# Expert up weights in two 4 MB loads instead of four of 2 MB

## The chip, the cores and the metric

The kernel runs on one core of one Trainium2 chip. The metric is device time in microseconds of one execution; before the change it is 2763.34 us, the median of three executions (2761.53 to 2763.45).

## What is computed

A first block of two layers (SwiGLU feed-forward, a mixer of convolution, gated recurrence and pooling, cross attention, a second feed-forward, a layer norm after each), then a second block of one layer, whose mixture of experts is the part that matters here. All is float32; T = 256 tokens, D = 1024, 32 experts of which each token uses 4. Cut to what matters:

```
h = layer_norm_2(DEEPNORM_ALPHA * h + y @ w_out, ln1_g, ln1_b)      # norm "A" in the kernel
# moe: router logits -> top 4 of 32 experts per token, softmaxed gates; for every expert e, on its tokens
hdn    = xb @ w_up[e] + b_up[e]                  # w_up[e]: 1024 x 2048, 8 MB
gate_h = minimum(hdn[:, :1024], 7);  up_h = clip(hdn[:, 1024:], -7, 7)
act    = (up_h + 1) * gate_h * sigmoid(1.702 * gate_h)
y      = (act @ w_down[e] + b_down[e]) * gate    # w_down[e]: 1024 x 1024, 4 MB
h = layer_norm_2(DEEPNORM_ALPHA * h + sum of y, ln2_g, ln2_b)       # norm "B"
h = h + sigmoid(h @ w_ple_gate + b_ple_gate) * (p @ w_ple)
```

## The kernel before

One program with a queue of instructions for each engine, tied by counting semaphores that the code writes out itself; nothing reorders them. SyncE (SP) issues nearly all loads, in the order in which they stand in its block. They land in a ring of 12 slots (`ring`, 8 KB per partition and slot, so 1 MB a slot): `loaded[s]` counts loads of slot s that landed, `used[s]` releases by the engine that read it. A load waits until its slot has been given back, and all that stands behind it on SP waits with it. `align()` moves on to slot 0.

Ahead of the experts the ring holds, in slots 0 to 5, the parameters of norm A (released by GpSimd), the router weights (TensorE), a table `tri` (VectorE, L1836), a table `before` (VectorE, at L1850, after the counting matmuls of L927), `b_up` (TensorE, L902) and `b_down` (TensorE, L915). Slots 6 to 11 are free long before.

Each expert then fills the ring exactly once: 8 slots for w_up, 4 for w_down. `load_pair` fills two adjacent slots with one transfer of 2 MB, in which each of the 128 partitions gets 16 KB that are adjacent in memory; it waits for both slots. Since partition p of k-tile pair j gets rows 256j + 2p and 256j + 2p + 1 of w_up, the other operand has to be cut the same way: `strip("A", k)` takes every second column of `hn` (transposes of norm A) and of `h` (the gather), and the router weights and the norm's gains and biases (`COLS_EVEN_ODD`) are laid out in the same order.

Every expert has room for 64 tokens (`few`, the branch that runs here; `many` is for fuller experts). TensorE's work for one expert, in order (counted as the trace does, which records each float32 matmul instruction twice): 64 up matmuls (L963), 8 for each slot k, with a wait for the transfer ahead of slots 0, 2, 4 and 6 and a release behind each slot; four transposes (L976); the gather of the next expert's tokens by a 0/1 matrix (32 matmuls, L935); four more transposes (L976); the combine of the previous expert's result (L944); two transposes of the gates (L990); 32 down matmuls (L1001), with waits ahead of slots 8 and 10. VectorE and ScalarE turn up into down's input between. After the last expert come the final combine, norm B, and a gate product with loads that follow the expert loads on SP.

Of the kernel before, what the change touches and what calls it, by code (L numbers as in the profile page):

```python
# [23 lines left out]
P = 128  # L24
# [3 lines left out]
DT = D // P  # L28
LAYERS = 2
FF = 2816  # L30
CH = 256
# [17 lines left out]
         ("conv_b_2", 8), ("lru_b_r_2", 8), ("lru_b_i_2", 8), ("lru_lambda_2", 8),  # L49
         ("gla_b_gate_2", 4), ("gla_norm_g_2", 2)]  # L50
COLS3 = [("ln2_g_2", 8), ("ln2_b_2", 8)]
COLS_EVEN_ODD = {"ln1_g_2": 0, "ln1_b_2": 4}


Q, K, PR, SU, FQ, FK, AA, AX_, V, Y = 0, 1024, 2048, 3072, 4096, 5120, 6144, 7168, 7680, 9728
# [99 lines left out]
def program(nc, book, a):  # L155

    book.iters = {}
    with ExitStack() as ctx:
# [11 lines left out]
        work_halves, at = {}, 0  # L170
        for off, size in sorted(((DH_, 2048), (HTH, 2048), (HDL, 1024), (HDH, 1024), (HTL, 2048), (GH_, 2048), (UH_, 2048))):
# [3 lines left out]
            at = off + size  # L175
# [74 lines left out]

        def col(name, i, n=1):

            if name in COLS_EVEN_ODD:
                at = 16 + 8 * (i % 2) + COLS_EVEN_ODD[name] + i // 2
                return cols[:, 2, at:at + 1]
            for b, group in enumerate((COLS1, COLS2, COLS3)):
                at = 0
                for nm, rows in group:
                    if nm == name:
                        if isinstance(i, int):  # L260
                            return cols[:, b, at + i:at + i + n]
                        return cols[:, b, bass.ds(i + at, n)]
                    at += rows
# [22 lines left out]
        def _(sp):  # L286
# [27 lines left out]
                plain(sp)  # L314
                sp.dma_start(dst, src).then_inc(loaded[s].sem, 16)

            def load_pair(name, second, src):

                s = pos[0] % RING
                pos[0] += 2  # L320
                loaded[s].add(name)
                for x, i in ((name, s), (second, s + 1)):
                    used[i].add(x)
                    slot_of[x] = i
                    sp.wait_ge(used[i].sem, used[i].at(x))
                    plain(sp)
                sp.dma_start(ring[:, s:s + 2, :].rearrange("p s n -> p (s n)"), src).then_inc(loaded[s].sem, 16)

            def align():
                pos[0] = -(-pos[0] // RING) * RING  # L330
# [115 lines left out]
            for j in range(4):  # L446
                load(f"w2o{j}", rows(wout2, 2 * j), "p (k n) -> p k n", k=2)
            ln_params(("lnp", "A"), a["ln1_g_2"], a["ln1_b_2"], 0)
            load("router", a["w_router_2"].rearrange("a (k p r) n -> p (a k) (r n)", p=P, r=2),
                 "p (k n) -> p k n", k=4)  # L450
            load("tri", a["c_tri"], None)
            load("before", a["c_moe"].rearrange("p a n -> p (a n)"), None)
            load("bup", a["b_up_2"].rearrange("a e (j n) -> (a e j) n", n=512), None)
            load("bdown", a["b_down_2"].rearrange("a e n -> (a e) n"), None, part=32)
            align()
            wup = a["w_up_2"].rearrange("a e (k p r) n -> p (a e) k (r n)", p=P, r=2)
            wdn = a["w_down_2"].rearrange("a e (j p r) n -> p (a e) j (r n)", p=P, r=4)
            with counted(book, sp, "e", EXPERTS, loaded + used) as e:
                for k in range(0, DT, 2):
                    load_pair(("moe", "u", k), ("moe", "u", k + 1), wup[:, e, k // 2, :])  # L460
                for j in range(0, 4, 2):
                    load_pair(("moe", "d", j), ("moe", "d", j + 1), wdn[:, e, j // 2, :])
            ln_params(("lnp", "B"), a["ln2_g_2"], a["ln2_b_2"], 0)
            load("ptok", a["p_2"].rearrange("l a (t p) n -> p (l a t) n", p=P), "p (t n) -> p t n", t=TT)
            load("wple", rows(a["w_ple_2"].rearrange("a k n -> (a k) n"), 0), "p (k n) -> p k n", k=2)
# [7 lines left out]
        def _(pe):  # L473
# [62 lines left out]

            def strip(tag, k):

                return bass.ds(CH * (k // 2) + k % 2, P, step=2) if tag == "A" else slice(k * P, k * P + P)

            def transposes(tag, src, ready):

# [136 lines left out]
            open_bank(0, "params")  # L679
            for b, n in enumerate((128, 102, 16)):  # L680
                pe.transpose(ps[:, 0, b * P:b * P + n], work[0:n, Y + b * P:Y + b * P + P], ident[0:n, 0:n])
            for r in range(2):
                mm = pe.transpose(ps[:, 0, 272 + 8 * r:280 + 8 * r], work[0:8, bass.ds(Y + 384 + r, P, step=2)],
                                  ident[0:8, 0:8])
            mm.then_inc(pe_full.add("params"), 1)

            with counted(book, pe, "L", LAYERS, emptied + [pe_full]) as L:
# [261 lines left out]
            def few():  # L949
                pe.wait_ge(h_ready.sem, h_ready.at(("h", "A")))  # L950
                pe.wait_ge(sel_ready.sem, sel_ready.at("sel0"))
                gather("xg0")
                with counted(book, pe, "few", EXPERTS, emptied + [pe_full], "e") as e:
                    def gate_up():

                        for x in range(2):
                            open_bank(x, ("gu", x))
                        pe.wait_ge(emptied[2].sem, emptied[2].at("xg"))
                        for k in range(DT):
                            s = arrived(("moe", "u", k)) if k % 2 == 0 else slot_of["moe", "u", k]  # L960
                            for x in range(2):
                                for lo, c0 in ((0, 0), (CAP, D)):
                                    mm = pe.matmul(ps[lo:lo + CAP, x, :],  # L963
                                                   work[:, XG + k * CAP:XG + k * CAP + CAP],
                                                   ring[:, s, c0 + 512 * x:c0 + 512 * x + 512],
                                                   start=(k == 0), stop=(k == DT - 1))
                                if k == DT - 1 and x == 0:
                                    mm.then_inc(pe_full.add(("gu", 0)), 1)
                            mm.then_inc(used[s].sem, 1)

                    def turned(x):

                        pe.wait_ge(emptied[x].sem, emptied[x].at(("gu", x), 1))
                        emptied[x].add(("gut", x))
                        for f in range(4):
                            mm = pe.transpose(ps[:, x, f * P:f * P + P],  # L976
                                              work[:, bass.ds(GUT + 512 * x + f, P, step=4)], ident[:])
                        mm.then_inc(pe_full.add(("gut", x)), 1)

                    gate_up()  # L980
                    turned(0)
                    pe.wait_ge(sel_ready.sem, sel_ready.at("sel"))
                    gather("xg")
                    turned(1)

                    combine("back")

                    open_bank(2, "GT")
                    for t in range(TT):
                        mm = pe.transpose(ps[:, 2, t * P:t * P + P], work[:, GG + t * P:GG + t * P + P], ident[:])  # L990
                    mm.then_inc(pe_full.add("GT"), 1)

                    open_bank(3, "y")
                    for j in range(4):
                        if j % 2 == 0:
                            pe.wait_ge(dve_done.sem, dve_done.at(("few", j // 2)))
                        s = arrived(("moe", "d", j)) if j % 2 == 0 else slot_of["moe", "d", j]
                        for kk in range(2):
                            f = 2 * j + kk
                            for half in range(2):  # L1000
                                mm = pe.matmul(ps[half * CAP:half * CAP + CAP, 3, :],  # L1001
                                               work[:, ACTS + f * CAP:ACTS + f * CAP + CAP],
                                               ring[:, s, kk * D + half * 512:kk * D + half * 512 + 512],
                                               start=(f == 0), stop=(f == DT - 1))
                        mm.then_inc(used[s].sem, 1)
                pe.wait_ge(emptied[3].sem, emptied[3].at("y", 1, few=EXPERTS - 1))
                combine("last")

            def many():
                with counted(book, pe, "many", EXPERTS, emptied + [pe_full], "e") as e:  # L1010
                    def gate_up(j):

                        for what, bank, c0 in (("g", 2 * (j % 2), 0), ("u", 2 * (j % 2) + 1, D)):
                            open_bank(bank, ("all", what, j))
                            for pt in range(2):
                                o = c0 + 512 * (j // 2) + 2 * (j % 2) + pt
                                for k in range(DT):
                                    s = slot_of["moe", "u", k]
                                    if (j, what, pt, k % 2) == (0, "g", 0, 0):
                                        arrived(("moe", "u", k))  # L1020
                                    mm = pe.matmul(ps[:, bank, pt * T:pt * T + T], ring[:, s, bass.ds(o, P, step=4)], hT[:, k, :],
                                                   start=(k == 0), stop=(k == DT - 1))
                                    if (j, what, pt) == (3, "u", 1):
                                        mm.then_inc(used[s].sem, 1)
                            if (j, what) != (3, "u"):
                                mm.then_inc(pe_full.add(("all", what, j)), 1)
# [60 lines left out]
        def _(act):  # L1087
# [24 lines left out]
                    row(nm, b, at)  # L1112
                    at += n

            for nm, at in COLS_EVEN_ODD.items():
                act.dma_start(work[at:at + 4, Y + 384:Y + 640], a[nm].rearrange("a (k n) -> (a k) n", n=CH))\
                    .then_inc(prm.add(("row", nm)), 16)
            row("ln2_g_2", 2, 0)
            row("ln2_b_2", 2, 8)
# [983 lines left out]
```

## Time and profile before

| what | us |
|---|---|
| median of three executions | 2763.34 |
| the profiled execution | 2764.23 |
| its span (first to last instruction) | 2762.4 |
| TensorE matmul busy | 2585.3 (94%) |
| VectorE, ScalarE, GpSimd busy | 855.3, 648.1, 147.4 |
| mean granted clock of TensorE | 0.964 |
| bytes read | 663.02 MB |

Durations below are of the profiled execution, and its own time is the one to hold them against; it was 0.89 us longer than the median. The page cuts the span into 40 equal slices of 69 us. TensorE's busy share is modelled, so a 9 doesn't say by itself that TensorE is the limit. A matmul group's mean (595 ns at L963) is longer than the distance between two starts, because they overlap in pairs; distances are read from start times.

### The profile page before, as it was taken

Reading aid. Unit: us, or ns where it says so; the run is one execution under the profiler, and the core shown is the slowest. Engines: PE = TensorE matmul, PEld = TensorE weight load, DVE = VectorE, ACT = ScalarE, POOL = GpSimd, SP = SyncE. Lnnn points to the kernel's source line nnn. Section 1 sums busy time; section 2 is a strip of 40 time slices with the busy share of each in tenths; the row PEclk is TensorE's granted clock in tenths of the full one; section 3 lists DMA queues with packets and bytes.
Section 4 is the critical chain, followed back from the end, with each engine's and each line's share of the span. In section 5 each row is a group of like instructions: output and inputs, shape, how many; then the busy total and the mean of one; then the engine's idle time right before and its main releaser. Section 6 shows DMA issues by size and latency. Waiting matters only on the chain. (4 is left out here: it accounts for less than half of the span.)

```text
span 2762.4 us, 34575 instructions
## 1 busy us (share of the span) xinstructions
PE 2585.3 (94%) x13461; PEld 1769.7 (64%) x13461; DVE 855.3 (31%) x1274; ACT 648.1 (23%) x799; POOL 147.4 (5%) x101
## 2 busy tenths in 40 slices
PE   7999998999899999889999897999999999999987
PEld 7997756699799785669976784444444444444433
DVE  4442321344444241234431535111111211211222
ACT  4330011233333101123312311121221221221211
POOL 0001300100100130110010101000000000000001
PEclk9999998999999999899999998899999999999997
DMA  8546332454554634245454410899999999999990
GB/s 301 183 152 198 122 122 77 141 187 158 185 187 156 206 122 137 77 137 183 152 168 127 150 62 31 338 428 428 429 428 428 429 428 428 429 428 428 429 416 16
DMA packets 215410, 665.27 MB, mean 241 GB/s; under 512 B 9841, under 2 KB 164207, under 8 KB 190752
## 3 DMA queue, kind: packets, MB, share of 16 engines
q1 hardware_dynamic: 214004, 662.78, 63.0%
q8 instruction: 61, 1.00, 0.2%
q10 hardware_dynamic: 1324, 1.31, 0.1%
q14 instruction: 21, 0.17, 0.0%
HBM read 663.02 MB, written 1.05 MB: 240 GB/s over the span
## 5 line engine op out<-in xcount | busy, mean ns | idle before, releaser
L495 PE MATMUL ps<-hT,ring 128*128 128x256 f32 x1920 | 443.4, 394 | 40.0 <-DVE hT L1490 13.4
L963 PE MATMUL ps<-ring,work 128*64 128x512 f32 x2048 | 453.1, 595 | 29.4 <-DMA ring<-in_w_up_dram 28.7
L579 PE MATMUL ps<-work_halves 128*128 128x256 f32 x2560 | 463.2, 283 | 0.0
L495 PEld LDWEIGHTS ps<-hT,ring 128*128 128x128 f32 x1920 | 378.5, 198 | 98.3 <-issue 30.1
L579 PEld LDWEIGHTS ps<-work_halves 128*128 128x128 f32 x2560 | 401.3, 192 | 3.8
L1540 DVE TENSOR_TENSOR ring_halves<-ring,work_halves 128x2048 fp32r<-128x2048 f32 x124 | 283.8, 2292 | 256.1 <-ACT work_halves L1147 256.1
L579 PE MATMUL ps<-work_halves,ring_halves 128*128 128x256 f32 x1280 | 361.9, 283 | 0.0
L963 PEld LDWEIGHTS ps<-ring,work 128*64 128x64 f32 x2048 | 144.9, 137 | 331.7 <-issue 261.6
L1097 ACT COPY work<-ps 128x512 f32<-128x512 f32 x161 | 94.0, 585 | 905.7 <-PE ps L963 398.2
L1147 ACT CAST work_halves<-ring 128x2048 fp32r<-128x2048 f32 x124 | 235.3, 1901 | 84.3 <-PE ps L592 84.3
L579 PEld LDWEIGHTS ps<-work_halves,ring_halves 128*128 128x128 f32 x1280 | 245.2, 192 | 0.0
L1001 PE MATMUL ps<-ring,work 128*64 128x512 f32 x1024 | 226.8, 595 | 2.0
L592 PE MATMUL ps<-work_halves 128*128 128x512 f32 x704 | 220.3, 394 | 0.0
L1887 DVE TENSOR_SCALAR work<-work 128x128 f32<-128x128 f32 x64 | 19.3, 343 | 613.0 <-PE ps L963 613.0
L1990 POOL TENSOR_TENSOR h<-hn,ring 128x1024 f32<-128x1024 f32 x20 | 47.4, 2371 | 2271.2 <-DVE hn L1527 2271.2
L1001 PEld LDWEIGHTS ps<-ring,work 128*64 128x64 f32 x1024 | 70.8, 137 | 137.4 <-issue 127.8
L592 PEld LDWEIGHTS ps<-work_halves 128*128 128x128 f32 x704 | 129.7, 188 | 27.2
L592 PE MATMUL ps<-ring_halves,work_halves 128*128 128x512 f32 x352 | 139.1, 395 | 0.0
L935 PE MATMUL ps<-work,h 128*128 128x64 f32 x1056 | 132.9, 286 | 2.6 <-DVE work L1873 2.6
L935 PEld LDWEIGHTS ps<-work,h 128*128 128x128 f32 x1056 | 130.0, 200 | 2.7 <-issue 2.7
L506 PE MATMUL ps<-ring,work 128*128 128x512 f32 x288 | 125.2, 594 | 0.9 <-issue 0.7
L506 PEld LDWEIGHTS ps<-ring,work 128*128 128x128 f32 x288 | 55.0, 192 | 68.9 <-issue 68.5
(262 smaller groups left out, 1959.1 us busy)
## 6 DMA issues: line engine op xcount, KB each, us to landing
ring<-in_w_up_dram SPq DMA_DIRECT2D x128, 2048.0 KB, 23.7
ring<-in_w_down_dram SPq DMA_DIRECT2D x64, 2048.0 KB, 19.4
ring<-in_w_in_dram SPq DMA_DIRECT2D x52, 1024.0 KB, 5.4
ring<-in_ffn_gate_dram SPq DMA_DIRECT2D x44, 1024.0 KB, 7.1
ring<-in_ffn_up_dram SPq DMA_DIRECT2D x44, 1024.0 KB, 9.6
ring<-in_ffn_down_dram SPq DMA_DIRECT2D x44, 1024.0 KB, 5.0
ring<-in_w_out_dram SPq DMA_DIRECT2D x12, 1024.0 KB, 5.0
ring<-in_ca_k_dram SPq DMA_DIRECT2D x8, 1024.0 KB, 6.9
```

The source lines that it names most:

```text
L495: mm = pe.matmul(ps[:, bank, pt * T:pt * T + T], ring[:, s, k * CH + pt * P:k * CH + pt * P + P], x[:, k, :], start=(k == 0), stop=(k == D ...
L506: mm = pe.matmul(ps[:, 4 + 2 * t + half, :], lhs(kk, t), ring[:, s, kk * D + half * 512:kk * D + half * 512 + 512], start=(is_first and kk ...
L579: mm = pe.matmul(ps[:, bank, pt * T:pt * T + T], wt, x[:, k, :], start=(k == 0 and n == 0), stop=(k == DT - 1 and n == 2))
L592: mm = pe.matmul(ps[:, 4 + 2 * t + half, :], x, wt, start=(is_first and n == 0), stop=(is_last and n == 2))
L935: mm = pe.matmul(ps[:, 2, k * CAP:k * CAP + CAP], h[:, t, strip("A", k)], work[:, GS + t * CAP:GS + t * CAP + CAP], start=(t == 0), stop=( ...
L963: mm = pe.matmul(ps[lo:lo + CAP, x, :], work[:, XG + k * CAP:XG + k * CAP + CAP], ring[:, s, c0 + 512 * x:c0 + 512 * x + 512], start=(k == ...
L1001: mm = pe.matmul(ps[half * CAP:half * CAP + CAP, 3, :], work[:, ACTS + f * CAP:ACTS + f * CAP + CAP], ring[:, s, kk * D + half * 512:kk * ...
L1097: nc.scalar.copy(dst, ps[:, bank, :]).then_inc(emptied[bank].sem, 1)
L1147: nc.scalar.copy(wr(at, SLOT), ring[:, s, :])\
L1540: v.tensor_tensor(ring_halves[s][:], ring[:, s, :], wr(at, SLOT).bitcast(F32), ALU.subtract)\
L1887: v.tensor_scalar(w(GG + t * P, P), w(IOTA, P), pos, gate, ALU.is_equal, ALU.mult)
L1990: link(g.tensor_tensor(h[:, t, :], hn[:, t, :], ring[:, s, 0:D], ALU.mult))
```

## The change

The up weights of an expert come in two transfers of 4 MB, each into four adjacent slots, 32 KB of adjacent memory per partition; partition p gets rows 512j + 4p to 512j + 4p + 3. `load_group` takes any number of slots and waits for all of them before it issues. The down weights stay at two transfers of 2 MB. TensorE waits for w_up ahead of slots 0 and 4 only; releases stay one per slot. All that follows w_up's order goes over to steps of four: the columns of `hn` and `h`, the router weights (rows of 512 instead of 256 bytes), and the norm's gains and biases, which come as 2 rows of 512 instead of 4 of 256 and are turned by four small transposes instead of two.

```diff
--- before.py
+++ after.py
@@ -49,7 +49,7 @@
          ("conv_b_2", 8), ("lru_b_r_2", 8), ("lru_b_i_2", 8), ("lru_lambda_2", 8),
          ("gla_b_gate_2", 4), ("gla_norm_g_2", 2)]
 COLS3 = [("ln2_g_2", 8), ("ln2_b_2", 8)]
-COLS_EVEN_ODD = {"ln1_g_2": 0, "ln1_b_2": 4}
+COLS_BY_FOUR = {"ln1_g_2": 0, "ln1_b_2": 2}
 
 
 Q, K, PR, SU, FQ, FK, AA, AX_, V, Y = 0, 1024, 2048, 3072, 4096, 5120, 6144, 7168, 7680, 9728
@@ -250,8 +250,8 @@
 
         def col(name, i, n=1):
 
-            if name in COLS_EVEN_ODD:
-                at = 16 + 8 * (i % 2) + COLS_EVEN_ODD[name] + i // 2
+            if name in COLS_BY_FOUR:
+                at = 16 + 4 * (i % 4) + COLS_BY_FOUR[name] + i // 4
                 return cols[:, 2, at:at + 1]
             for b, group in enumerate((COLS1, COLS2, COLS3)):
                 at = 0
@@ -314,17 +314,18 @@
                 plain(sp)
                 sp.dma_start(dst, src).then_inc(loaded[s].sem, 16)
 
-            def load_pair(name, second, src):
+            def load_group(names, src):
 
                 s = pos[0] % RING
-                pos[0] += 2
-                loaded[s].add(name)
-                for x, i in ((name, s), (second, s + 1)):
+                pos[0] += len(names)
+                loaded[s].add(names[0])
+                for i, x in enumerate(names, s):
                     used[i].add(x)
                     slot_of[x] = i
                     sp.wait_ge(used[i].sem, used[i].at(x))
                     plain(sp)
-                sp.dma_start(ring[:, s:s + 2, :].rearrange("p s n -> p (s n)"), src).then_inc(loaded[s].sem, 16)
+                sp.dma_start(ring[:, s:s + len(names), :].rearrange("p s n -> p (s n)"), src)\
+                    .then_inc(loaded[s].sem, 16)
 
             def align():
                 pos[0] = -(-pos[0] // RING) * RING
@@ -446,20 +447,20 @@
             for j in range(4):
                 load(f"w2o{j}", rows(wout2, 2 * j), "p (k n) -> p k n", k=2)
             ln_params(("lnp", "A"), a["ln1_g_2"], a["ln1_b_2"], 0)
-            load("router", a["w_router_2"].rearrange("a (k p r) n -> p (a k) (r n)", p=P, r=2),
-                 "p (k n) -> p k n", k=4)
+            load("router", a["w_router_2"].rearrange("a (k p r) n -> p (a k) (r n)", p=P, r=4),
+                 "p (k n) -> p k n", k=2)
             load("tri", a["c_tri"], None)
             load("before", a["c_moe"].rearrange("p a n -> p (a n)"), None)
             load("bup", a["b_up_2"].rearrange("a e (j n) -> (a e j) n", n=512), None)
             load("bdown", a["b_down_2"].rearrange("a e n -> (a e) n"), None, part=32)
             align()
-            wup = a["w_up_2"].rearrange("a e (k p r) n -> p (a e) k (r n)", p=P, r=2)
+            wup = a["w_up_2"].rearrange("a e (k p r) n -> p (a e) k (r n)", p=P, r=4)
             wdn = a["w_down_2"].rearrange("a e (j p r) n -> p (a e) j (r n)", p=P, r=4)
             with counted(book, sp, "e", EXPERTS, loaded + used) as e:
-                for k in range(0, DT, 2):
-                    load_pair(("moe", "u", k), ("moe", "u", k + 1), wup[:, e, k // 2, :])
+                for k in range(0, DT, 4):
+                    load_group([("moe", "u", k + r) for r in range(4)], wup[:, e, k // 4, :])
                 for j in range(0, 4, 2):
-                    load_pair(("moe", "d", j), ("moe", "d", j + 1), wdn[:, e, j // 2, :])
+                    load_group([("moe", "d", j), ("moe", "d", j + 1)], wdn[:, e, j // 2, :])
             ln_params(("lnp", "B"), a["ln2_g_2"], a["ln2_b_2"], 0)
             load("ptok", a["p_2"].rearrange("l a (t p) n -> p (l a t) n", p=P), "p (t n) -> p t n", t=TT)
             load("wple", rows(a["w_ple_2"].rearrange("a k n -> (a k) n"), 0), "p (k n) -> p k n", k=2)
@@ -536,7 +537,7 @@
 
             def strip(tag, k):
 
-                return bass.ds(CH * (k // 2) + k % 2, P, step=2) if tag == "A" else slice(k * P, k * P + P)
+                return bass.ds(512 * (k // 4) + k % 4, P, step=4) if tag == "A" else slice(k * P, k * P + P)
 
             def transposes(tag, src, ready):
 
@@ -679,9 +680,9 @@
             open_bank(0, "params")
             for b, n in enumerate((128, 102, 16)):
                 pe.transpose(ps[:, 0, b * P:b * P + n], work[0:n, Y + b * P:Y + b * P + P], ident[0:n, 0:n])
-            for r in range(2):
-                mm = pe.transpose(ps[:, 0, 272 + 8 * r:280 + 8 * r], work[0:8, bass.ds(Y + 384 + r, P, step=2)],
-                                  ident[0:8, 0:8])
+            for r in range(4):
+                mm = pe.transpose(ps[:, 0, 272 + 4 * r:276 + 4 * r], work[0:4, bass.ds(Y + 384 + r, P, step=4)],
+                                  ident[0:4, 0:4])
             mm.then_inc(pe_full.add("params"), 1)
 
             with counted(book, pe, "L", LAYERS, emptied + [pe_full]) as L:
@@ -957,7 +958,7 @@
                             open_bank(x, ("gu", x))
                         pe.wait_ge(emptied[2].sem, emptied[2].at("xg"))
                         for k in range(DT):
-                            s = arrived(("moe", "u", k)) if k % 2 == 0 else slot_of["moe", "u", k]
+                            s = arrived(("moe", "u", k)) if k % 4 == 0 else slot_of["moe", "u", k]
                             for x in range(2):
                                 for lo, c0 in ((0, 0), (CAP, D)):
                                     mm = pe.matmul(ps[lo:lo + CAP, x, :],
@@ -1016,7 +1017,7 @@
                                 o = c0 + 512 * (j // 2) + 2 * (j % 2) + pt
                                 for k in range(DT):
                                     s = slot_of["moe", "u", k]
-                                    if (j, what, pt, k % 2) == (0, "g", 0, 0):
+                                    if (j, what, pt, k % 4) == (0, "g", 0, 0):
                                         arrived(("moe", "u", k))
                                     mm = pe.matmul(ps[:, bank, pt * T:pt * T + T], ring[:, s, bass.ds(o, P, step=4)], hT[:, k, :],
                                                    start=(k == 0), stop=(k == DT - 1))
@@ -1112,8 +1113,8 @@
                     row(nm, b, at)
                     at += n
 
-            for nm, at in COLS_EVEN_ODD.items():
-                act.dma_start(work[at:at + 4, Y + 384:Y + 640], a[nm].rearrange("a (k n) -> (a k) n", n=CH))\
+            for nm, at in COLS_BY_FOUR.items():
+                act.dma_start(work[at:at + 2, Y + 384:Y + 896], a[nm].rearrange("a (k n) -> (a k) n", n=512))\
                     .then_inc(prm.add(("row", nm)), 16)
             row("ln2_g_2", 2, 0)
             row("ln2_b_2", 2, 8)
```

On SP, in the loop over experts (`in_w_up_dram` and `in_w_down_dram` are the weights in memory, `used0` to `used11` the releases of the slots), before and then after:

```order
L116 ISA
L327 ISA [waits used0,used1]
L327 DMA ring<-in_w_up_dram 128x4096
L327 ISA [waits used2,used3]
L327 DMA ring<-in_w_up_dram 128x4096
L327 ISA [waits used4,used5]
L327 DMA ring<-in_w_up_dram 128x4096
L325 REGISTER_ALU
L327 ISA [waits used6,used7]
L327 DMA ring<-in_w_up_dram 128x4096
L327 ISA [waits used8,used9]
L327 DMA ring<-in_w_down_dram 128x4096
```

```order
L116 ISA
L327 ISA [waits used0,used1,used2,used3]
L327 DMA ring<-in_w_up_dram 128x8192
L325 REGISTER_ALU [waits used4,used5]
L327 ISA [waits used6,used7]
L327 DMA ring<-in_w_up_dram 128x8192
L327 ISA [waits used8,used9]
L327 DMA ring<-in_w_down_dram 128x4096
```

Four issues of 4096 elements per partition became two of 8192, and the first of them waits for `used2` and `used3` too.

On TensorE, the up matmuls of one expert (`loaded0` and so on are the landed transfers; `work` holds the gathered tokens) up to the transposes behind them, before and then after:

```order
L963 MATMUL ps<-ring,work 64x512 [waits loaded0]
L963 MATMUL ps<-ring,work 64x512 x7
L486 ISA
L963 MATMUL ps<-ring,work 64x512 [waits loaded2]
L963 MATMUL ps<-ring,work 64x512 x7
L963 MATMUL ps<-ring,work 64x512 [waits loaded4]
L963 MATMUL ps<-ring,work 64x512 x7
L486 ISA
L963 MATMUL ps<-ring,work 64x512 [waits loaded6]
L963 MATMUL ps<-ring,work 64x512 x7
L976 MATMUL ps<-ident,work 128x128 [waits emptied0]
```

```order
L964 MATMUL ps<-ring,work 64x512 [waits loaded0]
L964 MATMUL ps<-ring,work 64x512 x15
L487 ISA
L964 MATMUL ps<-ring,work 64x512 [waits loaded4]
L964 MATMUL ps<-ring,work 64x512 x15
L977 MATMUL ps<-ident,work 128x128 [waits emptied0]
```

Since the trace records a float32 matmul twice, the 8 instructions between two waits are 16 matmuls of the trace (two slots), and the 16 are 32. The waits for slots 2 and 6 are gone, and twice as many matmuls stand behind the last one.

## Rows read from the trace of the kernel before

**Rows 1.** The page's 40 slices (each digit a busy share in tenths)

```profile
PE   7999998999899999889999897999999999999987
...
PEclk9999998999999999899999998899999999999997
DMA  8546332454554634245454410899999999999990
GB/s 301 183 152 198 122 122 77 141 187 158 185 187 156 206 122 137 77 137 183 152 168 127 150 62 31 338 428 428 429 428 428 429 428 428 429 428 428 429 416 16
```

**Rows 2.** Stretches of one expert each; last three columns: granted clock, DMA, GB/s

```profile
1779.18:1807.31 28.13, 28.07 (x149) 12.53 (x146) 5.35 (x16) 6.00 (x9) 0.00 (x0) 1.00 1.01 428
...
2627.59:2656.95 29.36, 28.29 (x149) 12.46 (x147) 5.35 (x16) 6.00 (x9) 0.00 (x0) 1.00 1.01 428
```

**Rows 3.** TensorE's waits, 1740 to 2690: us in total, times, longest

```profile
PE ps L963 <- DMA ring<-in_w_up_dram: 28.7, 29, 1.0
```

**Rows 4.** TensorE in order of time: start, us, what; in brackets idle before it

```profile
1749.28 15.67 PE L963 MATMUL ps<-ring,work 128*64 128x512 f32 x64 [0.76 <-ACT work L1097]
...
1779.18 13.90 PE L963 MATMUL ps<-ring,work 128*64 128x512 f32 x64
1793.02 0.75 PE L976 MATMUL ps<-ident,work 128*128 128x128 f32 x4
...
1800.39 7.09 PE L1001 MATMUL ps<-ring,work 128*64 128x512 f32 x32
1807.31 13.90 PE L963 MATMUL ps<-ring,work 128*64 128x512 f32 x64
...
2668.42 3.65 PE L963 MATMUL ps<-ring,work 128*64 128x512 f32 x16 [1.01 <-DMA ring<-in_w_up_dram]
2672.01 0.75 PE L976 MATMUL ps<-ident,work 128*128 128x128 f32 x4
...
2679.38 7.09 PE L1001 MATMUL ps<-ring,work 128*64 128x512 f32 x32
```

**Rows 5.** DMA packets in 1900:2600 (16 KB rows), 2680:2690 (4 KB), 1411:1415 (1 KB)

```profile
DMA packets 20596, 299.97 MB, mean 429 GB/s; under 512 B 2288, under 2 KB 2288, under 8 KB 2288
DMA packets 1091, 4.10 MB, mean 410 GB/s; under 512 B 66, under 2 KB 98, under 8 KB 1091
DMA packets 1384, 1.40 MB, mean 350 GB/s; under 512 B 17, under 2 KB 1384, under 8 KB 1384
```

**Rows 6.** Start of the stage: SP issues, VectorE's release, lone transfer's issue to landing

```profile
1714.18 26.91 SPq L327 DMA_DIRECT2D ring<-in_w_up_dram  x4
1738.90 0.22 DVE L1850 COPY work<-ps 128x64 f32<-128x64 f32 x1 [10.55 <-PE ps L927]
1739.36 0.34 SPq L327 DMA_DIRECT2D ring<-in_w_up_dram  x1
ring<-in_w_up_dram SPq DMA_DIRECT2D x1, 2048.0 KB, 7.7
```

**Rows 7.** Behind the experts: SP's last issues, and TensorE's first use

```profile
2665.80 12.25 SPq L315 DMA_DIRECT2D ring<-in_w_ple_gate_dram  x4
2716.98 30.29 PE L506 MATMUL ps<-ring,hT 128*128 128x512 f32 x64
```

**Rows 8.** Transposes on TensorE without a step, with step 2 and with step 4

```profile
1701.40 1.95 PE L550 MATMUL ps<-ident,hn 128*128 128x128 f32 x8 [3.36 <-DVE hn L1527]
1713.74 1.09 PE L902 MATMUL ps<-ident,ring 128*128 128x128 f32 x4
2694.80 1.09 PE L1060 MATMUL ps<-ident,ring 128*128 128x128 f32 x4 [5.66 <-issue]
2699.27 1.94 PE L550 MATMUL ps<-ident,hn 128*128 128x128 f32 x8 [3.38 <-DVE hn L1527]
2705.50 1.97 PE L550 MATMUL ps<-ident,hn 128*128 128x128 f32 x8 [4.29 <-DVE hn L1527]
```

**Rows 9.** The small transposes at the start, and the router's load and first use

```profile
20.08 0.38 PE L683 MATMUL ps<-ident,work 8*128 8x8 f32 x2
20.49 0.35 ACT L1216 COPY cols<-ps 128x230 f32<-128x230 f32 x1 [1.40 <-PE ps L683]
21.07 15.76 PE L495 MATMUL ps<-hT,ring 128*128 128x256 f32 x64 [0.61 <-ACT cols L1217]
1612.41 0.38 SPq L315 DMA_DIRECT2D ring<-in_w_router_dram  x1
1706.19 3.62 PE L896 MATMUL ps<-ring,hT 128*128 128x32 f32 x16
```

## The prediction

> **What bounds the kernel now.** I read the 40 slices of the page first. From slice 26 on, the DMA line stands at 9 and the GB/s line at 428 to 429 [rows 1]: this is the expert stage, the only part whose loads are resized. TensorE also stands at 9 there, so the slices don't say which of the two binds. The table by stretches does: early in the stage an expert takes 28.13 us from first up matmul to first up matmul, later 29.36 us, at the same DMA rate and the same granted clock of 1.00 [rows 2]. The list of waits shows what the 1.2 us are: 28.7 us of TensorE waiting for w_up in 29 of 32 experts [rows 3], always at the last quarter of the up matmuls, the 16 behind the wait for `loaded6` [rows 4]. So TensorE could do an expert in 28.13 us, and from the fourth one on it is paced by DMA: 12.58 MB (six transfers of 2 MB) at 428.6 GB/s are 29.36 us. DMA binds nearly the whole stage, with TensorE 1.2 us behind it; the other engines have cover.
>
> **What DMA time consists of.** Three stretches of back-to-back loads, each nearly pure in row size [rows 5]. Of an engine's time (16 engines): 11,200 us for 18,308 rows of 16 KB are 611.8 ns a row; 160 us for 993 rows of 4 KB, less 32 small ones (1.5 us), 159.6 ns; 64 us for 1,367 rows of 1 KB, 46.8 ns. The first two give 36.80 ns per 1,000 bytes (434.8 GB/s over 16 engines) and 8.9 ns that each row costs whatever its length. The third checks it: 37.7 + 8.9 = 46.6 against 46.8. The cost is tied to the row, not the transfer: a 2 MB transfer has 8 rows per engine, a 1 MB one of 4 KB rows 16, and the 8.9 ns fit both.
>
> **The change, part by part** (against the profiled execution: span 2762.4, time 2764.23 us, 0.89 us over the median of 2763.34).
>
> 1. Longer rows. Per expert and DMA engine 32 up rows of 16 KB become 16 of 32 KB. By the fit such a row takes 1205.8 + 8.9 = 1214.7 ns, against 2 x 611.8. Saved 16 x 8.9 = 0.142 us an expert; a period of 29.22 us, still over TensorE's 28.13. DMA stays the bound, so all of it counts: 32 x 0.142 = -4.6 us. Bounds: 0 (rows still cut at 16 KB) and -9.1 (no cost per row left on the up loads); -4.6 since a fit through three sizes says it.
>
> 2. The head start that is lost. Before, the first transfer needs only slots 0 and 1 and leaves at 1714.18, when the router matmuls have read slot 1. The next waits for slots 2 and 3, that is for the constant table `before`, which VectorE gives back at L1850 (1738.90 + 0.22); it leaves at 1739.36, and only then does DMA run without a break [rows 6]. So 2 MB are in early. After, the first transfer waits for slots 0 to 3 and leaves at 1739.36 with nothing done before. At 428.6 GB/s that puts 4.9 us of data into the bound stream: +4.9. It can't be less, unless DMA stops being the bound; TensorE needs the data at 1749.28, and 4 MB land at about 1739.36 + 7.7 + 4.9 = 1752.0 (7.7 us is what the lone 2 MB transfer took to land). These 2.7 us of TensorE waiting are not added: TensorE has a wait on DMA from the first expert on.
>
> 3. The tail behind the last up transfer. Now TensorE waits for the last 2 MB and then has 16 matmuls before the transposes at L976: 2668.42 to 2672.01. With 4 MB groups it waits for slots 4 to 7 and has 32. A matmul adds 13.84 / 64 = 0.216 us (1779.18 to 1793.02 for 64) [rows 4]; 16 more are +3.4. In the other 31 experts this lies inside the DMA period: after the wait TensorE does 6.9 + 7.3 + 7.0 us and then the first half of the next expert (6.9), 28.1 in all, against 29.22. Only the last one shows it. Its down weights land 4.9 and 9.8 us behind the last up transfer, and down starts 14.4 us after it; they are hidden. Landing of a 4 MB transfer may come up to one 16 KB row (0.6 us) later after its data; I take 0.
>
> 4. Ring turn-over. A group leaves when four slots are free. TensorE has eaten slots 0 to 3 by 12.3 us before DMA would want them for the next expert (it reads them from 9.8 to 16.7 of a 29.2 us period, plus 3 us of landing), slots 8 to 11 about 11 us before. SP has fewer instructions. So the stream doesn't break: 0. The last group is followed by the loads of the norm, `ptok` and the gate weights; the first use of the latter is at 2716.98, and they left from 2665.80 on [rows 7]: 30 us of cover.
>
> 5. Reads with step 4 instead of 2 (transposes of `hn`, gather from `h`). Transposes of `ring` with step 4 (L902) take 1.09 us for four, those without a step (L1060) 1.09, both at the low clock; the eight of `hn` with step 2 take 1.95, without one 1.94 and 1.97 [rows 8]. So 0. In the gather there are 1.09 us of slack per expert anyway.
>
> 6. Router rows of 512 instead of 256 bytes: issued at 1612.41 and used at 1706.19, 0. Four tiny transposes instead of two at the start (L683, two of 257 ns that start 0.1 apart), with ScalarE waiting for them and TensorE for its copy [rows 9]: 0.3 us at most, 0.2 taken.
>
> Sum: -4.6 + 4.9 + 3.4 + 0.2 = +3.9, so 2768.1 for an execution like the profiled one, 2767.3 as a median (+0.14%).
>
> The rows here say 8.9 ns per row. The Trainium skill (DMA: Bandwidth & Descriptors, "Why small descriptors are slow") names a fixed overhead of about 3 cycles per packet between the engine's read and write sides; with the 850 MHz of its Bandwidth section that is an estimate of 3.5 ns. By that item 1 would be -1.8 and the whole +6.7.
>
> **Rivals.**
> A. The rate doesn't rise: rows over 16 KB are cut in two, or what looks like a cost per row is something else. For: no row of more than 16 KB is in the trace. Against: the fit. Then items 2, 3 and 6 stand alone: +8.5, 2771.9. This is the slower side; the place is the 32 KB row, and it decides once less than 3.0 of the 4.6 us arrive.
> B. Part of the 8.9 ns grows with the row's bytes, so that two short rows save only half of it when they become one: -2.3 instead of -4.6, 2769.6. Against: the fit leaves 0.2 ns at 1 KB. The skill's 3 cycles would make it 2770.1.
> C. The rate rises more than by the fit, for instance because reads of 32 KB from HBM run better. Faster by 0.2% needs a period of 28.92 us, up loads at 438.5 GB/s; the fit has 434.8 as its end. Full gain: TensorE becomes the bound at 28.13 us (457 GB/s), the stage runs 1752.0 + 1.8 (slow clock in the first expert) + 32 x 28.13 = 2654, 32 us earlier: 2731. For it: only that the row is untried.
> D. The wider pitch hurts: an engine's and its neighbours' reads now lie 32 KB steps apart. 1% off the up loads costs 6.2 us; at the 410 GB/s of the 4 KB rows, 33 us: 2800; at 350, 146 us. Against: 1, 4 and 16 KB rows, at their different pitches, lie on one line. The skill's page on DMA ("Latency and other measured facts") reports such a loss for pitches of 2 MiB and no noticeable one at 512 KiB; by it nothing is lost here, and no run shows it.
> E. TensorE becomes the bound through step 4 in the gather: from 34 ns more for each of 32 matmuls. 64 ns would be 31 us. Item 5 speaks against.
>
> **How the numbers follow.** Forecast 0.58, A 0.20, B 0.03, C 0.09, D 0.07, E 0.03. A measurement of this kernel can't tell 0.2% (5.5 us) from no change, so "same" is 2757.8 to 2768.9. The forecast's own range, from the landing of larger transfers and the start, is 2765.5 to 2769.5: of its 0.58 I count 0.46 as same, 0.10 slower, 0.02 faster. With A, B, D and E slower is 0.43; with C faster is 0.11; same 0.46. The range of 8 in 10 takes in A and the mild end of C: 2761.8 to 2773.5.
>
> **What would show it.** Rows of 32 KB in the packet count: 32 data rows per engine and expert (16 long ones of up, 16 of down) where there were 48. A rate of about 430.6 GB/s and a period of 29.22 us (A: 428.6 and 29.36). First w_up issue at 1739.4 and first up matmul near 1752. One wait on w_up of some 1.1 us per expert, before the 33rd of 64 up matmuls. In the last expert 32 matmuls between that wait and the transposes. The forecast is wrong if waits on DMA vanish (C), if the period is over 29.4 (D), if the gather's mean of 281 ns rises (E), or if gaps appear in the DMA stream, which would mean that ring turn-over (item 4) fails.

## The result, and the profile after

The changed kernel takes 2921.93 us (median of four executions; 2921.70 to 2922.34) against 2762.44 us, the median of the kernel before over four executions: a ratio of 1.0579, 95% interval 1.0561 to 1.0597. That is 159 us slower, where 3.9 us were forecast; the step that failed is item 5 of the change, the reads with a step of 4.

The slices of the changed kernel's page, the lines that answer to [rows 1] (73 us each):

```profile
PE   8999998998999998899998969999999999999996
PEclk9999999999999999899999968998888888888887
DMA  8545332455455332354544019999998999999870
GB/s 285 188 153 192 130 101 95 165 187 188 159 187 179 132 134 89 130 173 144 175 137 140 28 65 418 376 370 373 374 373 353 366 372 369 372 374 372 360 320 15
```

From slice 26 on the loads run at 370 GB/s, not 428, and the granted clock stands mostly at 8 instead of 9. DMA is no longer the bound. TensorE's waits from 1740 to 2850 say the same, against [rows 3]:

```profile
PE ps L964 <- DMA ring<-in_w_up_dram: 3.9, 2, 2.5
```

Two waits on w_up in 32 experts, both in the first. TensorE in order of time, first the start of the stage, then one expert in the middle (start, us, what), against [rows 4]:

```profile
1741.92 7.70 PE L936 MATMUL ps<-work,h 128*128 128x64 f32 x32 [2.61 <-DVE work L1874]
1752.08 9.34 PE L964 MATMUL ps<-ring,work 128*64 128x512 f32 x32 [2.46 <-DMA ring<-in_w_up_dram]
1762.84 7.09 PE L964 MATMUL ps<-ring,work 128*64 128x512 f32 x32 [1.42 <-DMA ring<-in_w_up_dram]
...
2128.86 13.90 PE L964 MATMUL ps<-ring,work 128*64 128x512 f32 x64
2142.69 0.75 PE L977 MATMUL ps<-ident,work 128*128 128x128 f32 x4
2143.27 7.67 PE L936 MATMUL ps<-work,h 128*128 128x64 f32 x32
2150.74 1.06 PE L977 MATMUL ps<-ident,work 128*128 128x128 f32 x4
2151.74 3.78 PE L945 MATMUL ps<-work 64*128 64x512 f32 x8
2155.45 0.69 PE L991 MATMUL ps<-ident,work 128*128 128x128 f32 x2
2156.07 7.09 PE L1002 MATMUL ps<-ring,work 128*64 128x512 f32 x32
```

and the same stretch of an expert in the kernel before:

```profile
2025.99 0.75 PE L976 MATMUL ps<-ident,work 128*128 128x128 f32 x4
2026.58 3.93 PE L935 MATMUL ps<-work,h 128*128 128x64 f32 x32
2030.35 0.68 PE L976 MATMUL ps<-ident,work 128*128 128x128 f32 x4
2030.95 1.99 PE L944 MATMUL ps<-work 64*128 64x512 f32 x8
2032.87 0.44 PE L990 MATMUL ps<-ident,work 128*128 128x128 f32 x2
```

The up and down matmuls are as fast as before. Between them four pieces grew, read from start to start: the gather from 3.77 to 7.47 us, the second transposes from 0.60 to 1.00, the combine from 1.92 to 3.71, the gate transposes from 0.50 to 0.62. That is 6.01 us, and 28.13 + 6.01 = 34.14 is the new period (2128.86 to 2162.99: 34.13). Two causes stand in it, as the stretches of that expert show. They are the up matmuls, the gather to 2146, its rest, the second transposes and the combine, and down. Behind the length of the stretch stand the busy times of TensorE's matmuls, its weight loads, VectorE, ScalarE and GpSimd; the third column from the right is the granted clock:

```profile
2128.86:2142.69 13.83, 13.83 (x66) 4.43 (x63) 0.57 (x3) 2.46 (x3) 0.00 (x0) 1.00 1.00 411
...
2143.27:2146.00 2.73, 2.73 (x14) 2.73 (x13) 1.77 (x5) 0.12 (x1) 0.00 (x0) 0.96 0.97 420
2146.00:2150.74 4.74, 4.74 (x22) 4.74 (x22) 0.00 (x0) 0.00 (x0) 0.00 (x0) 0.50 0.99 429
2150.74:2155.45 4.71, 4.71 (x13) 1.84 (x14) 2.02 (x6) 2.70 (x4) 0.00 (x0) 0.50 1.03 445
2156.07:2162.99 6.92, 6.92 (x34) 2.37 (x35) 0.02 (x1) 0.37 (x1) 0.00 (x0) 1.00 0.49 163
```

The gather starts at the full 2.4 GHz and is slow from its first matmul. Some 3 us into it the clock falls to 0.50 (1.2 GHz), and stays low into the gate transposes (0.55 over 2155.45 to 2156.07). So 3.70 us are the gather's own and 2.31 us are what runs at the low clock behind it. In the kernel before the same stretches were granted 1.00 throughout. TensorE's matmuls are busy for the whole of each of these rows: the busy share doesn't tell a fast engine from one that waits for its operand.

### The profile page after: what moved, and what is told of

Read it like the earlier page. It is cut to its first block and busy times, and to the rows that moved or that the text cites. A ratio compares the mean times of both kernels' runs of the same rounds, so it can differ in the third digit from the quotient of the medians.

```text
span 2919.9 us, 34355 instructions
## 1 busy us (share of the span) xinstructions
PE 2772.6 (95%) x13463; PEld 1916.6 (66%) x13463; DVE 855.4 (29%) x1274; ACT 652.0 (22%) x799; POOL 147.5 (5%) x101
## 5 line engine op out<-in xcount | busy, mean ns | idle before, releaser
L936 PE MATMUL ps<-work,h 128*128 128x64 f32 x1056 | 253.4, 423 | 2.6 <-DVE work L1874 2.6
L936 PEld LDWEIGHTS ps<-work,h 128*128 128x128 f32 x1056 | 248.9, 329 | 2.7 <-issue 2.7
L945 PE MATMUL ps<-work 64*128 64x512 f32 x264 | 121.6, 1070 | 0.7 <-ACT work L1098 0.7
```

Of the source, the lines that this page charges most:

```text
L936: mm = pe.matmul(ps[:, 2, k * CAP:k * CAP + CAP], h[:, t, strip("A", k)], work[:, GS + t * CAP:GS + t * CAP + CAP], start=(t == 0), stop=( ...
L945: mm = pe.matmul(ps[:, 4 + 2 * t + half, :], work[lo:lo + CAP, GGT + t * P:GGT + t * P + P], work[lo:lo + CAP, YS:YS + 512], start=False, ...
```

## Experiments

**1. The gather's step alone.** In the kernel before, one line:

```diff
-                        mm = pe.matmul(ps[:, 2, k * CAP:k * CAP + CAP], h[:, t, strip("A", k)],
+                        mm = pe.matmul(ps[:, 2, k * CAP:k * CAP + CAP], h[:, t, bass.ds(512 * (k // 4) + k % 4, P, step=4)],
```

> The kernel before with one thing of the change: the gather reads its columns of h with a step of 4 elements (its result is another order of columns than the weights have; loads, waits and all else as before). Theory S (the step of the stationary reads is the cause): an expert takes about 34.1 us on TensorE as in the changed kernel, no waits on w_up, gather 7.5 us and combine 3.7 us instead of 3.8 and 1.9; the stage starts 2.8 us earlier than in the changed kernel, so about 2917 us. Theory L (the 4 MB loads with 32 KB rows, or their grouping, are the cause, and the slow gather comes from them): 2762 us, gather 3.8 us.

Measured: 2916.94 us, ratio 1.0559 (1.0543 to 1.0575). No wait on DMA is left, and an expert reads as in the changed kernel:

```profile
2171.45 7.67 PE L935 MATMUL ps<-work,h 128*128 128x64 f32 x32
2178.92 1.06 PE L976 MATMUL ps<-ident,work 128*128 128x128 f32 x4
2179.91 3.79 PE L944 MATMUL ps<-work 64*128 64x512 f32 x8
```

One operand's step, with all loads untouched, makes 153 of the 159 us. Theory L falls.

**2. The changed kernel without it.** The gather reads with step 2 again (`bass.ds(CH * (k // 2) + k % 2, P, step=2)`), the rest stays changed.

> The changed kernel with the gather's step set back to 2 (columns in another order than the weights have); loads in 32 KB rows, waits, router and norm order stay changed. Theory S: the forecast's sum then holds, 2767 us (2765 to 2770), period 29.22 us, one wait of 1.1 us on w_up per expert, DMA 430.6 GB/s. Theory L: about 2920 us.

Measured: 2764.28 us, ratio 1.0003 (0.9994 to 1.0012), no change that can be told, and 0.7 us under the range expected. TensorE at the end of the stage:

```profile
2640.66 7.09 PE L964 MATMUL ps<-ring,work 128*64 128x512 f32 x32 [0.78 <-DMA ring<-in_w_up_dram]
...
2669.87 7.09 PE L964 MATMUL ps<-ring,work 128*64 128x512 f32 x32 [0.78 <-DMA ring<-in_w_up_dram]
2676.89 0.75 PE L977 MATMUL ps<-ident,work 128*128 128x128 f32 x4
```

and its DMA packets in 1900:2600, which answer to the first of [rows 5]:

```profile
DMA packets 13808, 301.50 MB, mean 431 GB/s; under 512 B 1535, under 2 KB 1535, under 8 KB 1535
```

The period is 29.21 us (forecast 29.22), the rate 301.50 MB / 700 us = 430.7 GB/s (430.6), the wait on w_up ahead of the last 32 up matmuls 0.78 us (1.1), and 7.02 us lie between the last wait and the transposes where there were 3.59 (+3.4, item 3). In 700 us there are 12,273 data rows for 301.50 MB, 24.6 KB each: half 32 KB and half 16 KB, so rows of 32 KB aren't cut. Inside the stage items 1 to 4 hold. Executions also differ ahead of the stage; to leave that out, count from the first `b_down` matmul (L915, at 1729.40 in the kernel before, 1731.05 here) to the last combine (2687.16 and 2692.12): 957.76 and 961.07 us, 3.3 more, where items 1 to 3 sum to 3.7. Why the whole execution shows less stands below, under what the sum left out.

**3. Grouping or row length.** In the kernel before, up loads of 4 MB into four slots with rows of 16 KB:

```diff
-                for k in range(0, DT, 2):
-                    load_pair(("moe", "u", k), ("moe", "u", k + 1), wup[:, e, k // 2, :])
+                for k in range(0, DT, 4):
+                    load_group([("moe", "u", k + r) for r in range(4)], wup[:, e, k // 2:k // 2 + 2, :], rows=2)
```

The cut is to the up loads: `load_group` is the changed kernel's, `rows=2` cuts its destination into two rows per partition, and TensorE waits ahead of slots 0 and 4 only.

> The kernel before with up loads of 4 MB into four slots, but in rows of 16 KB (two per partition and transfer), all orders and steps as before. It separates the grouping from the row length. If a DMA row costs 8.9 ns whatever its length: 4.6 us more than the changed kernel with step 2, that is 2771 to 2772 us, period 29.36 us. If the cost belongs to the transfer and not to the row: the same as that kernel, 2767 us. If row length gives nothing, both are 2771.

Measured: 2769.33 us, ratio 1.0023 (1.0014 to 1.0033), 5.0 us over the kernel of experiment 2 on the same chip (4.6 expected), with a period of 29.37 us (2645.19 to 2674.56). That is 1.7 us under the total expected. The intervals of the two ratios don't meet. So the cost is tied to the row and not to the transfer, and the grouping alone costs 0.2%. Counted as above, the wait for the last up transfer ends 943.89 us after the first `b_down` matmul instead of 939.02 (+4.9, item 2), and the last combine starts 966.13 us after it instead of 957.76 (+8.4, items 2 and 3: 8.3).

**4. A cheap order for the gather.** GpSimd copies `h` into `hn` in the order of the weights once, after norm A, and the gather reads `hn[:, t, k * P:k * P + P]`. TensorE ahead of the first gather and VectorE ahead of norm B wait for the copy; the cut shows the copy alone:

```diff
+            pool.wait_ge(pe_full.sem, pe_full.at(("T", "A")))
+            for t in range(TT):
+                ins = g.tensor_copy(hn[:, t, :].rearrange("p (a r c) -> p a r c", a=2, r=4),
+                                    h[:, t, :].rearrange("p (a c r) -> p a r c", a=2, r=4))
+            done(ins, "perm")
```

> The changed kernel, but GpSimd copies h once into hn in the order of the weights (while it is otherwise idle, after norm A), and the gather reads the copy without a step. It computes all of the reference. Theory S: as with step 2, 2765 to 2770 us, gather 3.8 us, the copies hidden (GpSimd is idle from 1706 us on, first gather at 1742). Theory L: 2920 us.

Measured: 2762.65 us, ratio 0.9996 (0.9987 to 1.0005), 2.4 us under the range expected. The gather takes 3.57 us, and the copies are out of the way 28 us before it:

```profile
1709.62 3.92 POOL L2057 COPY hn<-h 128x1024 f32<-128x1024 f32 x2 [0.17 <-POOL h L1994]
```

This version computes all of the reference, with the changed loads, and has none of the loss.

**5 to 7. Which steps cost.** The kernel before with gather steps of 1, 3 and 8, one execution each.

> The kernel before with a gather that reads the columns of h without a step (the columns come in another order than the weights have). If the stationary operand is fetched in pieces of 16 bytes (theory P), a step of 1 touches 32 pieces per 128 columns, 2 touches 64, and both stay under what hides them: gather 3.6 to 3.8 us, time as before, 2763 us.

> The kernel before with a gather step of 3 elements (12 bytes; other columns than the weights have). Theory P: 96 pieces of 16 bytes per 128 columns, at the 1.82 ns a piece of step 4 (233 ns for 128) 175 ns a matmul, gather 5.6 us; TensorE's period then at least 29.9 us, over DMA's 29.36, 2780 us or more, and more if the clock falls too. Theory B (steps that are powers of two collide in some banks): step 3 as fast as 1, gather 3.8, 2763 us. Theory N (any step over 2 costs the full price): 7.5 us, 2917 us.

> The kernel before with a gather step of 8 elements (32 bytes; other columns than the weights have). Theory P: each column is a piece of its own already at step 4, so step 8 costs the same: gather 7.5 us, about 2917 us. Theory B or a price that grows with distance: over 10 us for the gather and over 3000 us in all.

Measured: 2756.65, 2832.91 and 2922.34 us, beside 2757.32 for one execution of the kernel before on that chip. One gather of 32 matmuls in the traces of steps 1, 3 and 8 (step 2 and 4 are above), each with the row behind it that ends it:

```profile
2166.27 3.73 PE L935 MATMUL ps<-work,h 128*128 128x64 f32 x32
2169.84 0.68 PE L976 MATMUL ps<-ident,work 128*128 128x128 f32 x4
```

```profile
2173.09 5.77 PE L935 MATMUL ps<-work,h 128*128 128x64 f32 x32
2178.69 0.78 PE L976 MATMUL ps<-ident,work 128*128 128x128 f32 x4
```

```profile
2178.13 7.86 PE L935 MATMUL ps<-work,h 128*128 128x64 f32 x32
2185.79 1.06 PE L976 MATMUL ps<-ident,work 128*128 128x128 f32 x4
```

| step (float32 elements) | 16-byte pieces per 128 columns | ns per matmul of the trace |
|---|---|---|
| 1 | 32 | 3.57 / 32 = 112 |
| 2 | 64 | 3.77 / 32 = 118 |
| 3 | 96 | 5.60 / 32 = 175 |
| 4 | 128 | 7.47 / 32 = 233 |
| 8 | 128 | 7.66 / 32 = 239 |

Step 3 came out at the 175 ns computed ahead, and step 8 costs what step 4 does. Banks that collide at powers of two, a single price for any step over 2, and a price that grows with distance are out. What fits the gather is a fetch in pieces of 16 bytes, one piece per 1.82 ns, hidden while a piece gives two columns. The 1.82 ns are taken from step 4; step 3 is the test of them. The Trainium skill (Advanced Engine Details and Errata, "SBUF Cachelines") has a rule of this form: 16-byte lines, at least two hits on a line to absorb the access latency. The gather's runs agree with it and put a price on it. The transposes don't: they read with step 4 at the full clock and start 0.12 us apart, half of the gather's 0.233 (rows in the next section). So the price isn't shown for every read with such a step, and why the transposes are spared stays open.

**8. Whose is the half clock.** The changed kernel with the combine ahead of the gather:

```diff
+                    combine("back")
                     gather("xg")
                     turned(1)
-
-                    combine("back")
```

> The changed kernel with the combine of the previous expert put ahead of the gather. It asks how much of the loss is the gather's own reads and how much the lower clock behind them. If the lower granted clock follows from the slow gather (theory C): the combine takes 1.9 us instead of 3.7, but what now follows the gather (transposes, gates, the first down matmuls) runs at the lower clock; between 2860 and 2925 us, the gather still 7.5. If the combine is slow for a reason of its own (its operands, the step-4 transposes before it): it takes 3.7 us there too.

Measured: 2985.43 us, one execution. The combine is back at its old speed; the gather and what follows are not:

```profile
2164.07 1.99 PE L945 MATMUL ps<-work 64*128 64x512 f32 x8
2165.99 7.73 PE L936 MATMUL ps<-work,h 128*128 128x64 f32 x32
2173.51 1.06 PE L977 MATMUL ps<-ident,work 128*128 128x128 f32 x4
2174.39 0.69 PE L990 MATMUL ps<-ident,work 128*128 128x128 f32 x2
2176.66 9.63 PE L1001 MATMUL ps<-ring,work 128*64 128x512 f32 x32 [1.57 <-DVE work L1904]
2186.12 13.90 PE L964 MATMUL ps<-ring,work 128*64 128x512 f32 x64
```

So the combine's slowness was the clock, and the low clock follows the gather (theory C). The total was missed, 60 us over the upper end: the combine had covered TensorE's wait for ScalarE and VectorE, which now shows (1.57 us ahead of down), and the low clock lasts into down (9.46 us instead of 6.92). The period is 36.56 us.

**9 and 10. Giving the head start back.** The six loads ahead of the experts move from slots 0 to 5 to slots 6 to 11 (`pos[0] += 6` ahead of norm A's parameters), first in the kernel before, then in the kernel of experiment 4.

> The kernel before with the six loads ahead of the experts (parameters of norm A, router, tri, before, b_up, b_down) in slots 6 to 11 instead of 0 to 5, so that slots 0 to 5 are free early and the first expert's loads don't wait for the table that is given back at 1739. It computes all of the reference. If the start of the unbroken DMA stream sets the end (item 2 of the forecast): the first expert is in before TensorE starts at 1749, the stream then begins when slots 0 and 1 come free, at 1755 with 31 experts to go, where the kernel before was at 1764.9: 9 to 10 us off, 2754 us. If the end hangs on something else: 2763 us.

> The same move of the six loads in the changed kernel with GpSimd's ordered copy of h (32 KB rows, gather without a step). It computes all of the reference. By the same sum the stream begins at 1759 (four slots must be free) with 31 experts at 29.22 us; the rows give back 4.4 us, the later start takes 3.5, the tail behind the last 4 MB 3.4: 2756 to 2757 us, 2 to 3 us behind the pairs, 7 us before the unmoved version. If the tail doesn't count it would be 2753.

Measured: 2755.07 us, ratio 0.9972 (0.9959 to 0.9984), and 2753.91 us, ratio 0.9969 (0.9957 to 0.9980). Both are about 0.3% under the kernel before; which is the better can't be told. The second was expected 2 to 3 us behind the first and isn't: in the traces both start the last combine 950.5 us after the first `b_down` matmul, where the kernel before takes 957.8. SP's issues in the trace of the first, which answer to [rows 6]:

```profile
1697.92 16.46 SPq L327 DMA_DIRECT2D ring<-in_w_up_dram  x4
1739.23 1.06 SPq L327 DMA_DIRECT2D ring<-in_w_down_dram  x2
1754.81 10.63 SPq L327 DMA_DIRECT2D ring<-in_w_up_dram  x4
```

All of the first expert's up loads have left by 1714.4, and the unbroken stream begins with the second expert at 1754.81. TensorE then waits for w_up in 22 experts instead of 29. Where the stream begins sets the end of a stage that DMA bounds, as item 2 has it.

## Why the prediction was wrong

- **Item 5, the reads with step 4, costed at 0: the step that failed.** Measured: +3.70 us per expert in the gather and +2.31 behind it. Less the 1.23 us of TensorE waiting that they absorb in 29 experts, that is 29 x 4.78 + 3 x 6.01 = 157 of the 159 us; the first up matmuls start 2.8 us later. It came about as rival E: TensorE became the bound through the gather. E had a chance of 0.03, and its example (64 ns more per matmul) was too small: it was 115 ns, and nothing in the sum was there for the clock.
- **The rows that item 5 read could not show it, for two reasons.** First, the clock: L902 and L1060 in [rows 8] are four transposes each at the low clock, and there the gather hides its step too. Its first run in the stage, all at 0.50, takes 7.06 us with step 2 and 7.70 with step 4, where at the full clock it takes 3.77 and 7.47 from start to start. Second, the kind of matmul: transposes don't carry this price at the full clock either. Eight transposes of `hn`, all at 1.00, without a step and with step 2 in the kernel before, then with step 4 in the changed one:

```profile
411.10 1.04 PE L550 MATMUL ps<-ident,hn 128*128 128x128 f32 x8
1696.93 1.11 PE L550 MATMUL ps<-ident,hn 128*128 128x128 f32 x8
```

```profile
1697.39 1.11 PE L551 MATMUL ps<-ident,hn 128*128 128x128 f32 x8
```

  Nor do the durations of the weight loads tell step 4 from step 2. In 1900:2600 of the kernel before L976 has step 4 and L990 none (min/median/max ns), but the eight `hn` loads with step 2 at L550 take 195/209/209 as well:

```profile
L976 PEld LDWEIGHTS ps<-ident,work x192: 195/210/242, 1908.5 to 2588.6; 128*128 128x128 f32 x192
...
L990 PEld LDWEIGHTS ps<-ident,work x48: 139/140/143, 1915.4 to 2590.9; 128*128 128x128 f32 x48
```

  The steps of 4 that the code of the kernel before writes out, in the branch that runs, are those of transposes (L902, L976). None of them is what the change made: a matmul other than a transpose with its stationary operand read with step 4. Item 5 was unmeasured, and 0 without a range was the mistake.
- **Item 1, longer rows, -4.6: right.** Period 29.21, rate 430.7, and 5.0 us between experiments 2 and 3. A fit through three row sizes carried over to an untried one. The lower price per row that the prediction sets beside it would have saved 1.8.
- **Item 2, the lost head start, +4.9: right.** The last up transfer is waited for 4.9 us later in experiment 3; experiment 9 moves the start of the stream and the time follows (7 us of the 9 expected). First up matmul at 1752.08, forecast 1752.0.
- **Item 3, the tail, +3.4: right**, 3.59 to 7.02 us in experiment 2.
- **Item 4: right** where DMA is the bound. The gaps in the DMA stream of the changed kernel are TensorE's lateness in giving slots back, not the grouping: experiment 1 has none of the grouping and the same pace.
- **Item 6** was not tested by itself.
- **What the sum left out.** Without item 5 it was +3.9; experiment 2 measured +0.7 with an interval of -1.7 to +3.3, though its stage came out as forecast. The rest lies behind the experts. TensorE idles between the last combine and the next transposes, for 5.66 us in the kernel before [rows 8], and for less in experiments 2 and 3:

```profile
2698.24 1.09 PE L1061 MATMUL ps<-ident,ring 128*128 128x128 f32 x4 [4.14 <-issue]
```

```profile
2702.52 0.66 PE L1064 MATMUL ps<-ident,ring 128*128 128x128 f32 x4 [3.73 <-issue]
```

  That gives back 1.5 and 1.9 us of what the stage lost, and the prediction has no term for it; what is left of the difference is within the interval. In experiment 10 it is 3.74 us against 5.80 in experiment 9. It is 3.7 to 4.1 us in the traces with wide steps and 2 MB loads too, so the grouping alone doesn't make it; what TensorE waits for there the trace doesn't show.
- **Rivals.** A is out (24.6 KB a row on average), B doesn't fit (half the saving would be 2.3 us, 5.0 were measured), D is out (the fitted rate was met to 0.1 GB/s), C did not happen, E did.

What stays open: why the clock falls in a slow gather and not in a fast one. It fell with steps 3, 4 and 8 (the combine behind step 3 took 3.44 us at 0.55) and stayed at 1.00 with steps 1 and 2; that the fall follows the gather is shown by experiment 8, what sets it off is not.

## What to carry to other kernels

When a layout change widens the step with which TensorE reads an operand, price that read by a row at the full clock with the same step, shape and kind of matmul, and multiply by its count before the slack is called enough; a transpose is no stand-in for another matmul. Where the trace has no such row, the term is unknown and not 0, and a kernel with that one line changed settles it, as experiment 1 did. In this gather two float32 values per 16 bytes cost almost nothing and one doubled the time; if the wide step can't be avoided, let an idle engine make one ordered copy outside the loop. In a stage that DMA bounds, look at when its unbroken stream begins: a small table in the wrong ring slot was worth 7 us, rows of twice the length 5.

## What the runs showed of the hardware

- The gather's float32 matmuls (stationary operand of 128 columns, 64 moving columns) start 112, 118, 175, 233 and 239 ns apart in the trace when the stationary operand is read with steps of 1, 2, 3, 4 and 8 elements. Transposes of 128x128 at the full clock settle at about 0.12 us apart with step 2 and with step 4.
- TensorE's granted clock can fall while TensorE is busy by the profile all the time: from 1.00 to 0.50 about 3 us into the gather shown of the changed kernel, and back to 1.00 in down. The slow operand thus costs a second time, 2.31 us on top of 3.70.
- A DMA row costs 8.9 ns beside its bytes at 434.8 GB/s, by a fit through rows of 1, 4 and 16 KB; with 32 KB rows for two thirds of the bytes the stream ran at the 430.7 GB/s that the fit gives (430.6).
